# Stage transposes of the first tile ahead of the last group, mixers begun tile by tile, last rows in two operations, last down matrices by output columns

## The chip, the cores and the metric

The kernel runs on one core of a Trainium2 chip. The metric is the device time of one execution in microseconds; the kernel before took 2252.16 us (median of three runs, 2251.80 to 2252.19). The profiled execution took 2251.79 us, and its span from first to last instruction is 2249.9 us.

## What is computed

The network works on 256 tokens of 1024 values, in float32. First comes one block with 16 extra tokens: a gated linear attention and a latent attention side by side, an output projection, then a layer of 64 experts with two chosen per token. After it come two more layers, each a mixer and two feed-forward networks (FFN) around layer norms:

```python
h = h + hier_moe(rmsnorm(h, ffn_norm[l]), ...)      # 64 experts, hdn = silu(xb @ w_gate[e]) * (xb @ w_up[e]); hdn @ w_down[e]
return rmsnorm(h, final_norm)[:, N_META:]
...
def layer_norm(x, g, b):
    mu = jnp.mean(xf, -1, keepdims=True)
    var = jnp.mean(jnp.square(xf - mu), -1, keepdims=True)
    y = (xf - mu) * lax.rsqrt(var + LN_EPS)
    return (y * g + b).astype(x.dtype)
def swiglu(x, w_gate, w_up, w_down):
    return (jax.nn.silu(x @ w_gate) * (x @ w_up)) @ w_down
```

The order is FFN 0, convolution mixer, FFN 1, FFN 2, mLSTM mixer, FFN 3. Each stage adds its output to a scaled residual and passes the sum through a layer norm. Each mixer has a cross-attention to 256 memory rows of its own, and its output projection takes the memory part and the mixer part together (`out_project`, four chunks of weights, the memory part's first).

## The kernel before, in words

The residual `h` stays on chip as two tiles of 128 tokens. Weights stream from HBM: in the expert layer into eight slots of 2 MB (`E.W`), afterwards into a ring of eight chunks of 1 MB (`X.ring`). SyncE issues all these loads in order; each waits until the chunk that used its slot is spent. Nothing is planned at run time: each engine has its instructions in the order of the source, and semaphores hold them together. A float32 matrix product counts as two instructions on TensorE in every view; a transpose counts as one.

**The expert layer** (L954 to L991) handles four experts at a time, 16 times: gate, up, down, then `combine`, which spreads the result to both token tiles. The last four down matrices arrive as four slices of the inner dimension (L99, L886), each 4 KB runs for the full 1024 output columns, and `out_of_slices` (L919) uses them as they land. ScalarE copies the result (L1048), TensorE combines it (L935), VectorE adds it to `h` (L1083), ScalarE squares and sums (L1656), VectorE scales (L2043). `early_sums` (L2032) makes VectorE form the first FFN's first two sets of weight sums ahead of the adds (L1784 to L1788, four operations each).

**A stage boundary** of stage j: VectorE adds TensorE's output to `h` and takes statistics (`merged`, L1721, after an FFN; `norm`, L1713, after a mixer), ScalarE takes the root (L1551), VectorE normalises the tile in two halves (`scaled`, L1687), TensorE transposes the eight 128 x 128 squares of the tile (`turn`, L1256), and VectorE and ScalarE each write four of them into `N.xT` with gain and bias (`spread`, L1695 and L1563). Only then does the next stage have its input. `rows` (L1708, L1709) applies gain and bias to `h` itself later.

**An FFN** (L1266) forms its products by seven products of half matrices instead of eight (p = 1 to 7), so it needs sums of weights (`weight_sums`) and of tokens (`token_sums`, L1802 to L1806, which need both tiles). Its order on TensorE: `turn(j, 0)`, `plain(0)` on tile 0 alone, `turn(j, 1)`, `plain(1)`, then wait for the token sums and `mixed(0)`. `plain` has 32 instructions, `mixed` 80. It ends with the down products; the last three chunks are taken product by product, in the order p = 1, 2, 6, 5, 3, 7, 4 (L1345). Tile 0 is complete with p = 3, tile 1 with p = 4.

**The mixers** wait for both tiles (`wait_x`, L1260), then run `group` (L1351): 32 instructions of 256 columns per chunk of weights. The mLSTM first has 32 narrow instructions for its gates (L1445). `out_project` (L1391) goes tile by tile and half by half through four chunks, 16 instructions each time. In the mLSTM, before it, 12 transposes (L1520) wait for VectorE's head norm, whose last input is the output gate that follows the last `token_group` (L1513).

## Time and profile before

| | |
|---|---|
| time, median of 3 | 2252.16 us |
| profiled execution | 2251.79 us, its span 2249.9 us |
| TensorE busy (PE) | 1843.9 us, 82% of the span |
| VectorE busy | 859.9 us, 38% |
| ScalarE busy | 214.2 us, 10% |
| chain that ended last | PE 62%, DMA 30%, SyncE's queue 3%, VectorE 3%, ScalarE 1% |
| longest in the chain | L1280 24%, L1307 11%, expert weights 10%, 10% and 9%, L1355 5% |

In a timeline row, the first number is the start in us from the start of the span, the second is how long the group lasts, and x says how many instructions it joins. What stands in brackets is how long the engine sat idle before it and what ended that. The clock column gives TensorE's granted clock as a share of 2.4 GHz: 1.00 is full, 0.50 is 1.2 GHz.

### The profile page before, as it was taken

The page shows a single profiled execution, that of the slowest core. Times are in us where ns is not written, and L with a number is a line of the kernel's source. Part 1 is how long each engine was busy: PE and PEld are TensorE (multiplying, and loading weights), DVE is VectorE, ACT ScalarE, POOL GpSimd, SP SyncE. Part 2 cuts the span into 40 slices and gives each one's busy share as a digit, 9 for nine tenths or more (in the row PEclk, how much of TensorE's full clock was granted, in tenths as well). Part 3 has the DMA queues.
Part 4 walks back from the last instruction along what each step waited for, and adds up shares of the span by engine and source line. Part 5 has one row for each costly group of instructions (what it writes and reads, how often), then busy time and mean ns, then how long its engine had stood idle before and what let it go on. Part 6 is the DMA issues. An engine that isn't in the chain of part 4 may idle for free.

```text
span 2249.9 us, 26172 instructions
## 1 busy us (share of the span) xinstructions
PE 1843.9 (82%) x11372; PEld 1225.0 (54%) x11372; DVE 859.9 (38%) x1804; ACT 214.2 (10%) x409; POOL 17.9 (1%) x41
## 2 busy tenths in 40 slices
PE   8997665566665556656699999999999999989997
PEld 6754232222222222212399658699579947859973
DVE  2223111111011111110276742476776755347675
ACT  2321000000000000000100011000010002201000
POOL 1100000000000000000000000000000000000000
PEclk9998887888887888777899999999999999999999
DMA  9268999999999999999955443365545444315540
GB/s 275 71 244 346 427 427 428 427 428 428 428 424 428 427 428 428 428 428 427 361 173 182 174 160 122 118 200 184 172 150 180 177 150 150 113 59 185 181 186 27
DMA packets 185419, 604.64 MB, mean 269 GB/s; under 512 B 17805, under 2 KB 139079, under 8 KB 161239
## 3 DMA queue, kind: packets, MB, share of 16 engines
q1 hardware_dynamic: 179680, 595.51, 68.4%
q10 hardware_dynamic: 5623, 7.42, 1.0%
q8 instruction: 92, 1.51, 0.3%
q14 instruction: 24, 0.20, 0.0%
HBM read 601.86 MB, written 1.05 MB: 268 GB/s over the span
## 4 chain that ended last, share of the span: by engine, by line
PE 62%; DMA 30%; SPq 3%; DVE 3%; issue 1%; ACT 1%; ACTq 0%; DVEq 0%
PE banks L1280 24%; PE banks L1307 11%; DMA e_W<-in_expert_w_up 10%; DMA e_W<-in_expert_w_down 10%; DMA e_W<-in_expert_w_gate 9%; PE banks L907 6%; PE banks L1355 5%; PE banks L915 3%; PE banks L1399 2%; PE banks L1475 2%; PE banks L203 2%; SPq L144 1%; SPq L887 1%; DMA x_ring<-in_ffn_w_up 1%; PE banks L398 1%
## 5 line engine op out<-in xcount | busy, mean ns | idle before, releaser
L907 PE MATMUL banks<-e_W,e_xT 128*32 128x512 f32 x2048 | 284.8, 716 | 176.5 <-DMA e_W<-in_expert_w_up 87.6
L907 PEld LDWEIGHTS banks<-e_W,e_xT 128*32 128x32 f32 x2048 | 79.4, 129 | 370.0 <-issue 368.7
L915 PE MATMUL banks<-e_W,e_hT 128*32 128x512 f32 x960 | 139.2, 745 | 140.0 <-DMA e_W<-in_expert_w_down 140.0
L1280 PE MATMUL banks<-x_xs,x_sums 128*128 128x128 f32 x2112 | 243.0, 275 | 0.0
L1280 PEld LDWEIGHTS banks<-x_xs,x_sums 128*128 128x128 f32 x2112 | 239.4, 192 | 0.0
L1280 PE MATMUL banks<-x_xT,x_ring 128*128 128x128 f32 x1408 | 169.0, 280 | 8.5 <-DVE x_xT L1695 6.8
L1280 PEld LDWEIGHTS banks<-x_xT,x_ring 128*128 128x128 f32 x1408 | 164.9, 196 | 9.5 <-DVE x_xT L1695 7.5
L915 PEld LDWEIGHTS banks<-e_W,e_hT 128*32 128x32 f32 x960 | 38.2, 133 | 230.3 <-issue 230.3
L1083 DVE TENSOR_TENSOR c_h<-c_h,banks 128x1024 f32<-128x1024 f32 x32 | 39.0, 1221 | 312.3 <-PE banks L935 312.3
L1307 PE MATMUL banks<-x_sums,x_hs 128*128 128x512 f32 x264 | 125.0, 592 | 0.0
L1355 PE MATMUL banks<-x_xT,x_ring 128*128 128x256 f32 x544 | 122.0, 386 | 1.6 <-DVE x_xT L1695 1.6
L1079 DVE TENSOR_TENSOR e_xT<-banks,e_fng 128x512 f32<-128x512 f32 x32 | 20.6, 686 | 255.5 <-PE banks L895 255.5
L1355 PEld LDWEIGHTS banks<-x_xT,x_ring 128*128 128x128 f32 x544 | 104.7, 194 | 17.4 <-DVE x_xT L1695 1.9
L1107 DVE TENSOR_TENSOR e_hid<-e_act,banks 128x512 f32<-128x512 f32 x16 | 11.0, 688 | 234.7 <-PE banks L907 234.7
L1280 PE MATMUL banks<-x_xT,x_sums 128*128 128x128 f32 x704 | 86.2, 276 | 2.6 <-DVE x_xs L1806 2.6
L1280 PE MATMUL banks<-x_xs,x_ring 128*128 128x128 f32 x704 | 85.8, 275 | 0.0
L1307 PEld LDWEIGHTS banks<-x_sums,x_hs 128*128 128x128 f32 x264 | 50.2, 190 | 63.1 <-issue 63.1
L1280 PEld LDWEIGHTS banks<-x_xT,x_sums 128*128 128x128 f32 x704 | 82.1, 192 | 3.4 <-DVE x_xs L1806 3.4
L1280 PEld LDWEIGHTS banks<-x_xs,x_ring 128*128 128x128 f32 x704 | 82.1, 192 | 0.0
L1307 PE MATMUL banks<-x_ring,x_hT 128*128 128x512 f32 x176 | 81.4, 592 | 0.0
L1824 DVE TENSOR_TENSOR x_us<-x_p,banks 128x256 f32<-128x256 f32 x44 | 18.5, 421 | 156.3 <-PE banks L1280 156.3
L935 PE MATMUL banks<-e_y,e_mixT 128*128 128x512 f32 x128 | 59.2, 605 | 18.3 <-ACT e_y L1048 17.1
(466 smaller groups left out, 2027.5 us busy)
## 6 DMA issues: line engine op xcount, KB each, us to landing
e_W<-in_expert_w_gate SPq DMA_DIRECT2D x64, 2048.0 KB, 21.7
e_W<-in_expert_w_up SPq DMA_DIRECT2D x64, 2048.0 KB, 20.7
e_W<-in_expert_w_down SPq DMA_DIRECT2D x64, 2048.0 KB, 20.2
x_ring<-in_ffn_w_gate SPq DMA_DIRECT2D x44, 1024.0 KB, 5.4
x_ring<-in_ffn_w_up SPq DMA_DIRECT2D x44, 1024.0 KB, 7.6
x_ring<-in_ffn_w_down SPq DMA_DIRECT2D x44, 1024.0 KB, 5.1
x_ring<-in_w_in_mlstm SPq DMA_DIRECT2D x13, 1024.0 KB, 5.2
x_ring<-in_w_in_conv SPq DMA_DIRECT2D x10, 1024.0 KB, 5.2
```

Source lines behind the costliest of these rows:

```text
L144: sp.dma_start(dst, src).then_inc(ld["params"], 16)
L203: i = pe.matmul(o, lhs(k), rhs(k), start=(k == 0), stop=(k == KD - 1))
L398: pe.matmul(ps[:, 4 + 2 * t + n, :], M.yT[:, k, t * P:(t + 1) * P], K.wout[:, k, n * 512:(n + 1) * 512], start=(k == 0), stop=False)
L907: i = pe.matmul(ps[SLOT * j:SLOT * (j + 1), b, :], E.xT[:, x, k, SLOT * j:SLOT * (j + 1)], E.W[:, slot0 + j, k * DE:(k + 1) * DE], start=( ...
L915: i = pe.matmul(ps[SLOT * j:SLOT * (j + 1), 2 + c, :], E.hT[:, f, SLOT * j:SLOT * (j + 1)], E.W[:, slot0 + j, f * D + c * 512:f * D + (c + ...
L935: i = pe.matmul(ps[:, 6 - 2 * t + c, :], E.mixT[:, x, t, :], E.y[:, c * 512:(c + 1) * 512], start=True, stop=True)
L1083: return v.tensor_tensor(K.h[:, t, :], K.h[:, t, :], ps[:, 6 - 2 * t:8 - 2 * t, :].rearrange("p b n -> p (b n)"), ALU.add)
L1280: mm = pe.matmul(ps[:, bank, lo + which * P:lo + (which + 1) * P], a, b, start=(k == 0), stop=(k == 3))
L1307: mm = pe.matmul(ps[:, DB[p], :], a, b, start=(c == 0), stop=(c == NFC - 1))
L1355: mm = pe.matmul(ps[:, bank, f2 * S:(f2 + 1) * S], w8(i)[:, k, f2 * P:(f2 + 1) * P], N.xT[:, k, :], start=(k == 0), stop=(k == KD - 1))
L1399: mm = pe.matmul(yb(t, m), X.mixT[:, 2 * kk + k2, t * P:(t + 1) * P], w2(at + n)[:, k2, m * 512:(m + 1) * 512], start=(n == 0 and k2 == 0) ...
L1475: mm = pe.matmul(ps[:, bank, t * FC:(t + 1) * FC], N.xT[:, k, t * P:(t + 1) * P], w8(i)[:, k, :], start=(k == 0), stop=(k == KD - 1))
```

## The change

- `expert_chunk`: each of the last four down loads covers two of the four inner slices and half of the output columns, as two transfers with runs of 2 KB. `out_of_slice` finishes columns 0 to 511 first; copy, `combine_half`, add and square follow per half. `early_sums` is gone; those two sets of weight sums now stand behind `spread(0, 0)` and `spread(0, 1)`.
- `turn` of the next stage's tile 0 stands ahead of the very last down product (FFN) or ahead of the last quarter of the output projection (mixers). VectorE's order follows: `spread(j, 0)` before the last add. It works for FFNs 0 to 2.
- `conv` and `lstm` start with `tile_group` on tile 0 (32 instructions of 128 columns), then transpose tile 1, then do the second half. The gates go tile by tile too.
- `out_project` is split: `out_memory` (the memory part, 16 instructions for all four outputs) and `out_rest` (48). In the mLSTM `out_memory` stands ahead of the 12 transposes.
- `last_rows` replaces `scaled` and `rows` at the end: two operations on each half of a tile, each half stored at once.
- Six more products on the identity in the front, after the first transposes; the gate bias is loaded with two transfers.

```diff
-        return K.dram["expert_w_down"][0, QUAD * q:QUAD * (q + 1)].rearrange("e (p k) n -> p e k n", p=P)[:, :, j % QUAD, :]
+        return K.dram["expert_w_down"][0, QUAD * q:QUAD * (q + 1)].rearrange("e (p k) n -> p e k n", p=P)[:, :, 2 * (j % 2):2 * (j % 2) + 2, 512 * (j % QUAD // 2):512 * (j % QUAD // 2 + 1)]
...
+        for n in range(WARM // 2):
+            pe.matmul(ps[:, 7, 0:P], K.ident[:, :], K.ident[:, :], start=True, stop=True)
...
-                out_of_slices(at + 2 * QUAD)
+                pe.wait_ge(self.mix_out, QUADS)
+                for m in range(2):
+                    for f2 in range(2):
+                        out_of_slice(at + 2 * QUAD + 2 * m + f2, m, f2)
+                    pe.wait_ge(self.y_out, q + m + 1)
+                    combine_half(q % 2, m)
+                return
...
                     for c in range(NFC - TAIL, NFC):
                         if p == 6:
                             wait_down(c)
+                        if p == 4 and c == NFC - 1 and n < 3:
+                            turn(j + 1, 0)
                         down(c, p)
...
+            def out_rest(at, tail, j):
+                for t in range(TT):
+                    for m in range(2):
+                        if t == 1 and m == 1:
+                            turn(j, 0)
+                        for n in range(1, 4):
...
             def conv():
                 at = AT_CONV
-                for k in (0, 4):
-                    wait_x(1, k)
-                group(at, 0)
+                first_tile(1)
+                tile_group(at, 0, 0)
+                turn(1, 1)
+                both_tiles(1)
+                tile_group(at, 0, 1).then_inc(s["spent"], 1)
...
             def lstm():
+                first_tile(4)
+                gates(0)
+                tile_group(at, 1, 0)
+                turn(4, 1)
+                both_tiles(4)
+                gates(1)
+                tile_group(at, 1, 1).then_inc(s["spent"], 1)
...
                 pe.wait_ge(ls["va"], 3)
+                pe.wait_ge(ls["hv"], 1)
+                out_memory(at + 13, 1)
                 for t in range(TT):
                     pe.wait_ge(ls["y"], t + 1)
...
             def norm(j, scale, last):
+                summed(j, 0, 0, scale, last)
+                summed(j, 0, 1, scale, last)
                 scaled(j, 0)
-                sums(j, 1, scale, last)
+                summed(j, 1, 0, scale, last)
                 spread(j, 0)
+                summed(j, 1, 1, scale, last)
                 scaled(j, 1)
                 spread(j, 1)
...
                 v.bn_aggr(N.mv[:, 0, :], N.stats[:, 0, :, :]).then_inc(s["mv"], 1)
+                if j < 6:
+                    scaled(j, 0)
+                else:
+                    last_rows(0)
                 got(6)
                 after(z)
                 z = add(1, 1, prod(7))
-                scaled(j, 0)
                 y = add(1, 0, prod(7))
-                after(z)
-                stats(1, 1)
+                if j < 6:
+                    spread(j, 0)
                 v.wait_ge(s["spent"], last)
                 after(y)
-                c(add_last(1, 0, prod(4), scale))
+                x = add(1, 0, prod(4))
+                stats(1, 1)
+                after(x)
...
+            def last_rows(t):
+                v.wait_ge(moe.ld_rows, 16 + 32 * 6)
+                v.wait_ge(s["root"], TT * 5 + t + 1)
+                c(v.reciprocal(N.root[:, t:t + 1], N.root[:, t:t + 1]))
+                cols = [slice(m * 512, (m + 1) * 512) for m in range(2)]
+                centred = [K.vc.mark(v.scalar_tensor_tensor(out=h[:, t, m], in0=h[:, t, m], scalar=N.mv[:, t, 0:1], in1=N.g[:, m],
+                                                            op0=ALU.subtract, op1=ALU.mult)) for m in cols]
+                for m, n in zip(cols, centred):
+                    v.wait_ge(K.vc.sem, n)
+                    v.scalar_tensor_tensor(out=h[:, t, m], in0=h[:, t, m], scalar=N.root[:, t:t + 1], in1=N.b[:, m],
+                                           op0=ALU.mult, op1=ALU.add).then_inc(s["rows"], 1)
...
             spread(0, 0)
+            v.wait_ge(moe.spent, XCHUNKS)
+            weight_sums(0, 0)
             spread(0, 1)
+            weight_sums(0, 1)
```

## Rows read from the trace of the kernel before

**Rows 1.** Chain that ended last, in order of time: start us, us, what
```profile
1126.56 130.69 PE banks L1280 x1168
...
1353.82 3.65 PE banks L1363 x16
...
1357.47 14.01 PE banks L1355 x64
...
1411.77 27.48 PE banks L1399 x64
...
1451.33 130.69 PE banks L1280 x1168
...
1894.40 3.65 PE banks L1363 x16
...
2041.68 130.69 PE banks L1280 x1168
```

**Rows 2.** One line of the program (L1256, stage transposes): idle TensorE time, us and times
```profile
  DVE c_h L1687: 13.5, 7
```

**Rows 3.** Timeline around the second FFN's end: start us, us, engine line op tiles [idle before]
```profile
1645.37 2.74 PE L1307 MATMUL banks<-x_sums,x_hT 128*128 128x512 f32 x6
...
1646.37 1.00 DVE L1687 TENSOR_SCALAR c_h<-c_h,n_mv,n_root 128x512 f32<-128x512 f32 x2
...
1647.95 1.04 PE L1256 MATMUL banks<-c_ident,c_h 128*128 128x128 f32 x8
...
1649.02 1.50 ACT L1563 ACTIVATE x_xT<-banks,n_lnT 128x128 f32<-128x128 f32 x4 [4.03 <-PE banks L1256]
...
1651.42 3.84 PE L1280 MATMUL banks<-x_xT,x_ring 128*128 128x128 f32 x32 [2.44 <-DVE x_xT L1695]
...
1655.10 1.04 PE L1256 MATMUL banks<-c_ident,c_h 128*128 128x128 f32 x8
...
1660.45 1.72 PE L1280 MATMUL banks<-x_xT,x_sums 128*128 128x128 f32 x13 [0.75 <-DVE x_xs L1806]
```

**Rows 4.** Busy time per stretch (PE, PEld, DVE, ACT, POOL), TensorE clock, DMA share, GB/s
```profile
1330.00:1332.00 2.00, 1.94 (x5) 1.62 (x6) 1.97 (x3) 0.00 (x0) 0.00 (x0) 0.50 1.12 351
...
1862.00:1864.00 2.00, 1.04 (x5) 0.64 (x3) 1.77 (x5) 0.92 (x3) 0.00 (x0) 0.50 1.10 347
...
2032.00:2034.00 2.00, 2.00 (x12) 2.00 (x11) 0.07 (x1) 0.00 (x0) 0.00 (x0) 0.51 1.11 353
```

**Rows 5.** Timeline, transposes of tile 0 ahead of the convolution and the mLSTM
```profile
1323.18 1.04 PE L1256 MATMUL banks<-c_ident,c_h 128*128 128x128 f32 x8
...
1857.08 1.04 PE L1256 MATMUL banks<-c_ident,c_h 128*128 128x128 f32 x8
```

**Rows 6.** Timeline, before the mLSTM's output projection
```profile
1980.30 0.64 DVE L2012 BATCH_NORM_AGGREGATE x_hmv<-x_hst 128x2 f32<-128x6 f32 x8
...
1996.75 2.79 PE L1520 MATMUL banks<-c_ident,x_pad 128*128 128x128 f32 x12 [7.51 <-DVE x_pad L2021]
...
1999.58 0.69 DVE L2024 COPY x_mixT<-banks 128x512 f32<-128x512 f32 x1 [0.26 <-PE banks L1520]
```

**Rows 7.** Timeline: three VectorE operations in a row; last one of the kernel
```profile
1316.26 1.89 DVE L1722 SCALAR_TENSOR_TENSOR c_h<-x_ud,c_h 128x512 f32<-128x512 f32 x3
...
2245.61 1.22 DVE L1709 TENSOR_TENSOR c_h<-c_h,x_b 128x1024 f32<-128x1024 f32 x1
```

**Rows 8.** Clock, DMA share, GB/s: w_out (4 KB rows), w_kv (2 KB rows)
```profile
52.00:54.00 2.00, 1.00 1.01 412
...
98.00:100.00 2.00, 1.00 1.04 393
```

**Rows 9.** Timeline, end of the expert layer
```profile
1100.75 3.33 PE L924 MATMUL banks<-e_W,e_hT 128*32 128x512 f32 x16 [3.18 <-DMA e_W<-in_expert_w_down]
...
1109.06 2.34 DVE L1083 TENSOR_TENSOR c_h<-c_h,banks 128x1024 f32<-128x1024 f32 x2
...
1115.35 6.38 PE L1280 MATMUL banks<-x_xT,x_ring 128*128 128x128 f32 x32 [1.71 <-DVE x_xT L1697]
```

More of the change, by code:

```diff
@@ L1110, in vector @@
             if q == QUADS - 1:
-                early_sums()
+                for m in range(2):
+                    cols = slice(m * 512, (m + 1) * 512)
+                    for t in range(TT):
+                        v.wait_ge(self.c_mm, TT * (q + m) + t + 1)
+                        v.tensor_tensor(K.h[:, t, cols], K.h[:, t, cols], ps[:, 6 - 2 * t + m, :], ALU.add).then_inc(self.summed, 1)
+                return
             for t in range(TT):
@@ L1245, in _ @@
             for t in range(TT):
-                sp.wait_ge(s["rows"], 7 * TT - TT + t + 1)
-                sp.dma_start(out[t * P:(t + 1) * P, :], h[:, t, :]).then_inc(s["stored"], 16)
-            sp.wait_ge(s["stored"], 16 * TT)
+                for m in range(2):
+                    sp.wait_ge(s["rows"], 6 * TT + 2 * t + m + 1)
+                    sp.dma_start(out[t * P:(t + 1) * P, m * 512:(m + 1) * 512], h[:, t, m * 512:(m + 1) * 512]).then_inc(s["stored"], 16)
+            sp.wait_ge(s["stored"], 16 * 2 * TT)
         @block.tensor
@@ L1357, in group, with tile_group @@
                 mm.then_inc(s["spent"], 1)
+            def tile_group(i, bank, t):
+                if t == 0:
+                    wait_chunk(pe, i)
+                for f2 in range(2):
+                    for k in range(KD):
+                        mm = pe.matmul(ps[:, bank, f2 * S + t * P:f2 * S + (t + 1) * P], w8(i)[:, k, f2 * P:(f2 + 1) * P],
+                                       N.xT[:, k, t * P:(t + 1) * P], start=(k == 0), stop=(k == KD - 1))
+                return mm
             def scores(layer):
@@ L1389, in turn_o, with out_part, out_memory @@
                 i.then_inc(xs["xy_mm"], 1)
-            def out_project(at, tail):
+            def out_part(at, n, t, m):
+                for k2 in range(2):
+                    mm = pe.matmul(yb(t, m), X.mixT[:, 2 * OUT_K[n] + k2, t * P:(t + 1) * P], w2(at + n)[:, k2, m * 512:(m + 1) * 512],
+                                   start=(n == 0 and k2 == 0), stop=(n == 3 and k2 == 1))
+                if t == 1 and m == 1:
+                    mm.then_inc(s["spent"], 1)
+                elif n == 3:
+                    mm.then_inc(s["bank"], 1)
+            def out_memory(at, layer):
+                wait_chunk(pe, at)
+                pe.wait_ge(xs["xy_out"], layer + 1)
                 for t in range(TT):
                     for m in range(2):
-                        for n, kk in enumerate(OUT_K):
+                        out_part(at, 0, t, m)
+            def out_rest(at, tail, j):
+                for t in range(TT):
+                    for m in range(2):
+                        if t == 1 and m == 1:
+                            turn(j, 0)
+                        for n in range(1, 4):
                             if t == 0 and m == 0:
@@ L1525, in tail @@
                         pe.wait_ge(ls["y_out"], TT)
-                out_project(at + 13, tail)
+                out_rest(at + 13, tail, 5)
             front.tensor(pe)
@@ L1530, in _ @@
             ffn(0, 0)
-            for t in range(TT):
-                turn(1, t)
             conv()
@@ L1535, in _ @@
             ffn(2, 3)
-            for t in range(TT):
-                turn(4, t)
             lstm()
@@ L1653, in _ @@
             moe.scalar(a)
-            for t in range(TT):
-                a.wait_ge(moe.summed, TT * (QUADS - 1) + t + 1)
-                K.ac(a, a.activation(N.junk[:, :], h[:, t, :], ACT.Square, accum_out=N.ss[:, t:t + 1]))
-                a.activation(N.root[:, t:t + 1], N.ss[:, t:t + 1], ACT.Sqrt, bias=K.eps[:, 0:1], scale=1.0 / D).then_inc(s["sumsq"], 1)
             spread(0, 0)
@@ L1702, in rows @@
                 for t in range(TT):
[L1703 to L1706 removed]
+                    v.wait_ge(s["turned"], 4 * j + 2 * t + 2)
                     if j:
@@ L1761, in merged @@
                 if j < 6:
-                    spread(j, 0)
-                scaled(j, 1)
-                if j < 6:
+                    scaled(j, 1)
                     spread(j, 1)
+                else:
+                    last_rows(1)
+            def last_rows(t):
[9 more added lines that the diff above has]
+                                           op0=ALU.mult, op1=ALU.add).then_inc(s["rows"], 1)
             def add_last(t, m, x, scale):
@@ L2051, in _ @@
             ffn(3, 5)
-            rows(6)
         @block.gpsimd
```

135 lines of the change are left out of this document (69 added, 66 removed).

## The prediction

> **What bounds the kernel now.** I read the chain of work that ended last first, because it says which engine sets the end in each stage. Up to 1089 us it is the stream of expert weights. From there on it is TensorE almost without a break, in long pieces such as the 130.69 us of FFN products [rows 1]. So the kernel can only be shortened where that chain of products is cut: at the stage boundaries and before the mLSTM's projection. The view of one line of the program says what the stage transposes waited for: 13.5 us of idle TensorE time in front of them, ended by VectorE's normalisation [rows 2]. The timeline shows how a boundary looks. After FFN 1 the last product row (p = 4) starts at 1645.37, the transposes of tile 0 at 1647.95, ScalarE's spread ends at 1650.52, and `plain(0)` starts only at 1651.42, because VectorE did tile 1's sums before its own spread [rows 3]. The last view is the one by stretches: at three of the boundaries the granted clock was 0.50 of 2.4 GHz [rows 4], so a boundary costs more than its idle time.
>
> **The units.** A 512-column instruction takes 27.48 / 64 = 0.43 us, so one down product (two instructions) takes 0.86 us and an output projection 27.5 us [rows 1]. A `group` of 32 instructions with 256 columns takes 14.01 / 2 = 7.0 us [rows 1]. 32 instructions with 128 columns take 3.65 us: 1651.42 to 1655.10 [rows 3] is that with the turn to the next work. So `tile_group` twice costs 7.3 us where `group` cost 7.0: splitting a group costs only 0.3 us. From the start of a `turn`, with the spreads free to run, to the end of ScalarE's spread it is 1650.52 - 1647.95 = 2.57 us, and I take 2.62 until TensorE goes on [rows 3]. From `turn(j, 1)` to `mixed(0)` it is 1660.45 - 1655.10 = 5.35 us [rows 3], set by spread and token sums and unchanged.
>
> **FFN 1 to FFN 2.** Call the old start of tile 0's transposes A. In the new order they start at A - 0.86, ahead of the last product, which then runs beside the spread. They wait for `scaled(j, 0)`. VectorE now does it as soon as the root is there and no longer after an add, and even in the old order it began at 1646.37, in two halves of 0.5 us [rows 3]. The transposes would start at 1647.09, and the second half is ready about 1646.5. The new wait is covered by about 0.6 us; if it were late, only the last product and the spread would queue behind it. `plain(0)` then starts at A - 0.86 + 2.62 = A + 1.76 instead of A + 3.47. Gain **1.7 us**. Tile 1 is late next: add, two statistics, root, scaling end about 7.9 us after 1645.37, and its transposes come 8.1 us after it, so they do not wait.
>
> **FFN 0 to the convolution.** A is 1323.18 [rows 5]. First half at A + 1.76, then 3.65, the turn of tile 1 with its wait 2.62, second half 3.65, two groups 13.96: the memory scores start at A + 25.64 = 1348.8. Before they started at 1353.82 [rows 1]. Gain **5.0 us**, of which about 3.1 us is the clock: the first fifteen instructions ran at 1.2 GHz [rows 4]. I take it that the new waits (0.7 and 1.6 us instead of 3.1 and 1.6) leave the clock at 2.4 GHz.
>
> **FFN 2 to the mLSTM.** A is 1857.08 [rows 5]. A + 1.76, then gates and `tile_group` of tile 0 (3.65 each; the trace has the gates only at 256 columns, and their 32 instructions cannot take longer than those of `tile_group`), 2.62, again 3.65 twice, two groups 13.96: the scores start at A + 32.9 = 1890.0 instead of 1894.40 [rows 1]. Gain **4.4 us**, some 2.9 of it clock [rows 4]. `rows(4)` on VectorE starts later but is over before the first queries are wanted.
>
> **Convolution to FFN 1.** The projection's work stays (27.5). Tile 0's transposes (1.04) stand in it, waiting for a normalisation that has a whole quarter (12 x 0.43 = 5.2 us) against the 3.7 us it needs. Then `plain(0)` 3.75 and 5.35 follow without a gap: 37.6 us from 1411.77, where it was 1451.33 - 1411.77 = 39.56 [rows 1]. Gain **2.0 us**.
>
> **The end of the mLSTM** is the largest term. TensorE sat idle 7.51 us in front of the 12 transposes, which took 2.79 us at half clock [rows 6]. `out_memory` is 16 x 0.43 = 6.9 us of work that fits into this gap, from 1989.24 to 1996.1. Its new wait on the head statistics is over at 1980.94 [rows 6]. The transposes start at 1996.75 as before, since the head norm hangs on the last `token_group` alone, and last 1.6 us. VectorE's copies, which ended at 1999.58 + 1.0 [rows 6], end about 1999.9; before, the memory part covered them, now TensorE waits some 1.5 us. Then 48 x 0.43 = 20.6, transposes 1.0, `plain(0)` 3.75, 5.35: `mixed(0)` at 2030.6 instead of 2041.68 [rows 1]. Gain **11.0 us**: 6.9 for the filled gap, 2.2 for clock up to 2001, 1.6 for clock in `plain(0)` [rows 4], 1.9 for the boundary, less 1.5 for the uncovered copies.
>
> **The end.** VectorE's last operation ended at 2245.61 + 1.22 = 2246.83 [rows 7]. Two operations on halves replace two on halves and two on whole tiles, and tile 0 no longer stands behind tile 1. Three such operations lasted 1.89 us, so four take 2.5 [rows 7]. `last_rows(0)` now delays tile 1's adds: its statistics are complete about 1.0 us later (2241.5), root and reciprocal 0.55, four operations 2.5: 2244.6. Gain 2.2; storing halves makes the last transfer half as large, up to 0.7 more. I take **2.7 us**.
>
> **The end of the expert layer.** The pieces become 2 KB instead of 4 KB. 4 KB rows moved at 412 GB/s and 2 KB rows at 393 [rows 8], a mean of 388 with the stretch after it; for 8.4 MB I add 1.4 us, between 0 and 2.5. By the Trainium skill (DMA: Bandwidth & Descriptors, Specifications) pieces from 512 B on reach line rate; then these 1.4 us are not paid and the total is 2223.9. In the other direction the work behind the last slice is halved: it ended with VectorE's adds at 1109.06 + 2.34 = 1111.40 [rows 9]. Now: products until 1104.1 + 1.4 [rows 9], copy of half the columns about 0.65, four products 1.9 with their latency, an add 0.7: 1108.8, so `plain(0)` starts 2.6 us earlier, at 1112.75 instead of 1115.35 [rows 9]. But the weight sums that ran during the wait for the last slice now stand behind the spreads. The first set (four operations, 2.6 by [rows 7]) hides behind `plain(0)`; the second stands between spread and token sums and delays `mixed(0)` by 2.6. The two cancel: gain **0.0**. With `plain(0)` at full clock instead of 1.2 GHz (6.38 us against 3.75) it is 2.6 more. With a drop caused by the new wait of 2.5 us before `mixed(0)` it is about 3 less.
>
> **At nothing:** the six products in the front (what follows waits for parameters until 47 us), the bias transfers, the earlier memory part in the convolution.
>
> Sum: 1.7 + 5.0 + 4.4 + 2.0 + 11.0 + 2.7 + 0.0 = 26.8 us. 2251.79 - 26.8 = 2225.0; the median of the runs is 0.37 higher, so **2225.3 us**.
>
> **The rivals.**
> *The clock still falls* at the two mixer starts. For it: it fell in [rows 4] after boundaries with 2.2 to 3.1 us of idle time, and 1.6 us remain, with 1.04 us of transposes before them. Against it: the boundary of [rows 3] had 2.44 us idle after transposes and ran on at full speed. Price 3.1 + 2.9: 2231.3 us. The Trainium skill (TensorE: Matmul & The Clock Gate, Part 4) says transposes do not count as busy time; by that the pause at tile 1's turn is 2.7 us and not 1.6, which is the argument for this rival. Chance 0.12.
> *The expert tail keeps its clock*, 2222.7 us: chance 0.15. *It loses it before `mixed(0)`*, 2228.3 us: chance 0.18. Both come from the same row [rows 9].
> *The memory part does not fill the gap*, because the head norm moves with it: 2232.2 us. Against it: no operation of that norm reads what `out_memory` writes. Chance 0.04.
> *Slower than before:* SyncE cannot feed eight transfers of 4096 pieces fast enough, and the last slice lands late. Everything behind it moves by the same amount, so this decides from 26.8 us on: 8.4 MB in 48 us, 175 GB/s. The 2 KB row at 393 speaks against it [rows 8]. At 160 GB/s the kernel would take 2256 us. Chance 0.03, with 0.01 for a loss that just cancels the gain.
>
> **How the numbers follow.** The forecast as it stands has 0.47, with 2 us either way for the small terms. The range 2221 to 2231.5 takes in the two cases of the expert tail and most of the first rival. A measurement of this kernel tells 0.2%, 4.5 us, from no change. All cases but the last give more than that: faster 0.96, same 0.01, slower 0.03.
>
> **What would show it.** TensorE's idle time before the 12 transposes of L1520 falls from 7.5 to under 1 us and they last 1.6; the clock stays at 1.00 in the first 10 us of both mixers; `plain(0)` follows the last output quarter without a gap; the last VectorE operation ends some 2.2 us earlier against p = 4's start; `mixed(0)` of FFN 0 starts within 1 us of 1126.6. The prediction is wrong if the new turns wait for VectorE, or if a 128-column half takes clearly more than 3.7 us.

## The result, and the profile after

The changed kernel takes **2218.66 us** (median of four runs, 2217.18 to 2219.77), the kernel before beside it 2252.18 us (2251.80 to 2252.26). The ratio is 0.985, with a 95% interval from 0.984 to 0.9864. That is 33.5 us faster; 26.8 were forecast, and 2218.66 lies 2.3 us below the low end of the range. The profiled execution took 2217.64 us with a span of 2215.9 us, 34.0 us less than the span before.

The chain of work that ended last, in order of time, of the kernel after (start us, us, what):

```profile
1122.20 130.69 PE banks L1322 x1168
...
1344.64 3.65 PE banks L1416 x16
...
1402.60 22.32 PE banks L1446 x52
...
1439.70 130.69 PE banks L1322 x1168
...
1647.15 130.69 PE banks L1322 x1168
...
1873.39 3.65 PE banks L1416 x16
...
2009.25 130.69 PE banks L1322 x1168
```

L1322 is `mixed(0)`, L1416 the memory scores, L1446 the output projection. Set against [rows 1] these starts cut the 34.0 us into parts. The start of `mixed(0)` in FFN 2 before was 1660.45 [rows 3].

| stretch | before | after | gain | forecast |
|---|---|---|---|---|
| start to `mixed(0)` of FFN 0 | 1126.56 | 1122.20 | 4.4 | 0.0 |
| to the convolution's scores | 227.26 | 222.44 | 4.8 | 5.0 |
| to its output projection | 57.95 | 57.96 | 0.0 | 0 |
| to `mixed(0)` of FFN 1 | 39.56 | 37.10 | 2.5 | 2.0 |
| to `mixed(0)` of FFN 2 | 209.12 | 207.45 | 1.7 | 1.7 |
| to the mLSTM's scores | 233.95 | 226.24 | 7.7 | 4.4 |
| to `mixed(0)` of FFN 3 | 147.28 | 135.86 | 11.4 | 11.0 |
| to the end of the span | 208.22 | 206.65 | 1.6 | 2.7 |

Two terms are far off: the expert tail (4.4 us too little) and the mLSTM's start (3.3 too little). The others differ by +0.5, +0.4, 0.0, -0.2 and -1.1.

The timeline of the kernel after at the start of the mLSTM (start us, us, engine line op tiles, idle time before in brackets):

```profile
1842.92 1.04 PE L1296 MATMUL banks<-c_ident,c_h 128*128 128x128 f32 x8
...
1843.79 1.02 PE L1349 MATMUL banks<-x_sums,x_hT 128*128 128x512 f32 x2
...
1845.64 1.92 PE L1507 MATMUL banks<-x_xT,x_wgate 128*4 128x128 f32 x32 [0.83 <-ACT x_xT L1631]
...
1847.49 3.84 PE L1408 MATMUL banks<-x_xT,x_ring 128*128 128x128 f32 x32
...
1851.16 1.04 PE L1296 MATMUL banks<-c_ident,c_h 128*128 128x128 f32 x8
...
1853.89 1.92 PE L1507 MATMUL banks<-x_xT,x_wgate 128*4 128x128 f32 x32 [1.69 <-ACT x_xT L1631]
```

The transposes (L1296) wait for nothing, the last down product (L1349) runs beside the spread, and the two waits that remain are 0.83 and 1.69 us. But the gates (L1507) take 1.92 us a tile, where the forecast had 3.65. The same timeline before the mLSTM's output projection:

```profile
1968.12 7.03 PE L1446 MATMUL banks<-x_ring,x_mixT 128*128 128x512 f32 x16
1975.76 1.74 PE L1592 MATMUL banks<-c_ident,x_pad 128*128 128x128 f32 x12 [0.61 <-DVE x_pad L2102]
1978.77 7.53 PE L1446 MATMUL banks<-x_ring,x_mixT 128*128 128x512 f32 x17 [1.26 <-DVE x_mixT L2106]
```

Where TensorE sat idle for 7.51 us [rows 6] it now does the memory part, and the 12 transposes take 1.74 us in place of 2.79. The view by stretches shows the clock there and at both mixers (columns as in [rows 4]):

```profile
1318.00:1320.00 2.00, 1.87 (x11) 1.04 (x9) 1.70 (x6) 0.96 (x3) 0.00 (x0) 1.00 0.72 217
1324.00:1326.00 2.00, 1.33 (x13) 1.09 (x11) 1.07 (x4) 0.63 (x2) 0.00 (x0) 1.00 1.04 351
1330.00:1332.00 2.00, 2.00 (x15) 1.84 (x14) 1.82 (x3) 0.00 (x0) 0.00 (x0) 1.00 0.04 8
1850.00:1852.00 2.00, 2.00 (x20) 1.96 (x19) 0.20 (x1) 0.00 (x0) 0.00 (x0) 1.00 1.10 349
...
1976.00:1978.00 2.00, 1.51 (x12) 1.04 (x10) 1.90 (x4) 0.00 (x0) 0.00 (x0) 1.00 0.72 204
```

All are at 1.00, full speed; the slow stretches of [rows 4] were at 0.50 and 0.51. At the convolution the two waits that remain are 0.78 and 1.69 us:

```profile
1320.65 3.81 PE L1408 MATMUL banks<-x_xT,x_ring 128*128 128x128 f32 x32 [0.78 <-DVE x_xT L1760]
...
1327.02 3.81 PE L1408 MATMUL banks<-x_xT,x_ring 128*128 128x128 f32 x32 [1.69 <-ACT x_xT L1631]
```

### The profile page after: what moved, and what is told of

Its sections match the earlier page's. It is cut to its first block, busy times and chain, and to the rows that moved or that the text cites. A ratio compares the mean times of both kernels' runs of the same rounds, so it can differ in the third digit from the quotient of the medians.

```text
span 2215.9 us, 26410 instructions
## 1 busy us (share of the span) xinstructions
PE 1828.5 (83%) x11480; PEld 1219.8 (55%) x11480; DVE 860.1 (39%) x1806; ACT 216.1 (10%) x416; POOL 17.8 (1%) x41
## 4 chain that ended last, share of the span: by engine, by line
PE 63%; DMA 29%; SPq 4%; DVE 2%; issue 1%; ACT 1%; DVEq 0%; ACTq 0%
PE banks L1322 24%; PE banks L1349 12%; DMA e_W<-in_expert_w_gate 10%; DMA e_W<-in_expert_w_down 9%; DMA e_W<-in_expert_w_up 9%; PE banks L913 7%; PE banks L1399 5%; PE banks L921 3%; PE banks L1446 2%; PE banks L1545 2%; PE banks L203 2%; SPq L144 1%; SPq L893 1%; SPq L891 1%; PE banks L1408 1%
## 5 line engine op out<-in xcount | busy, mean ns | idle before, releaser
L1322 PE MATMUL banks<-x_xs,x_sums 128*128 128x128 f32 x2112 | 243.0, 275 | 0.0
L1322 PEld LDWEIGHTS banks<-x_xs,x_sums 128*128 128x128 f32 x2112 | 239.4, 192 | 0.0
L1322 PE MATMUL banks<-x_xT,x_ring 128*128 128x128 f32 x1408 | 166.2, 277 | 2.1 <-DVE x_xT L1762 1.3
L1322 PEld LDWEIGHTS banks<-x_xT,x_ring 128*128 128x128 f32 x1408 | 162.5, 194 | 4.1 <-DVE x_xT L1760 1.6
L1349 PE MATMUL banks<-x_sums,x_hs 128*128 128x512 f32 x264 | 125.0, 592 | 0.0
L1399 PE MATMUL banks<-x_xT,x_ring 128*128 128x256 f32 x480 | 105.2, 380 | 0.0
L1399 PEld LDWEIGHTS banks<-x_xT,x_ring 128*128 128x128 f32 x480 | 90.6, 190 | 12.6 <-issue 0.7
L1322 PE MATMUL banks<-x_xT,x_sums 128*128 128x128 f32 x704 | 86.2, 276 | 4.5 <-DVE x_xs L1887 4.5
L1322 PE MATMUL banks<-x_xs,x_ring 128*128 128x128 f32 x704 | 85.8, 275 | 0.0
L1322 PEld LDWEIGHTS banks<-x_xT,x_sums 128*128 128x128 f32 x704 | 82.1, 192 | 5.3 <-DVE x_xs L1887 5.3
L1349 PEld LDWEIGHTS banks<-x_sums,x_hs 128*128 128x128 f32 x264 | 50.2, 190 | 63.1 <-issue 63.1
L1322 PEld LDWEIGHTS banks<-x_xs,x_ring 128*128 128x128 f32 x704 | 82.1, 192 | 0.0
L1349 PE MATMUL banks<-x_ring,x_hT 128*128 128x512 f32 x176 | 81.4, 592 | 0.0
## 6 DMA issues: line engine op xcount, KB each, us to landing
e_W<-in_expert_w_up SPq DMA_DIRECT2D x64, 2048.0 KB, 21.3
e_W<-in_expert_w_down SPq DMA_DIRECT2D x60, 2048.0 KB, 21.3
```

What stands on the lines that cost most here:

```text
L1322: mm = pe.matmul(ps[:, bank, lo + which * P:lo + (which + 1) * P], a, b, start=(k == 0), stop=(k == 3))
L1349: mm = pe.matmul(ps[:, DB[p], :], a, b, start=(c == 0), stop=(c == NFC - 1))
L1399: mm = pe.matmul(ps[:, bank, f2 * S:(f2 + 1) * S], w8(i)[:, k, f2 * P:(f2 + 1) * P], N.xT[:, k, :], start=(k == 0), stop=(k == KD - 1))
```

## The experiments

Twelve series of runs were made: ten kernels that differ from the changed one or from the one before by a single piece (one of them by two), one of these a second time, and the changed kernel again. Each stands beside the kernel before on the same chip (2251.8 to 2252.4 us in the median). Where a distance in a trace is given, it comes from one profiled execution of each kernel. "Landing" is the start of the products of the last down slice. Nothing of the computation is left out in any of them.

### The gates without alternating strips

`gates` writes its two halves to partitions 0 to 3 and 32 to 35, and takes them in turn. One edit puts the two halves one behind the other:

```diff
                 def gates(t):
-                    for k in range(KD):
-                        for f2 in range(2):
+                    for f2 in range(2):
+                        for k in range(KD):
```

> The changed kernel, with one loop order turned round: the mLSTM's gate products of a tile do all eight inner slices for the input gates (output rows 0 to 3) and then all eight for the forget gates (rows 32 to 35), where the changed kernel alternates between the two. Theory: they took 1.92 us for 32 instructions because neighbours in the queue write different row strips and run side by side; in a row on one strip they take 3.65 us for each tile, 3.5 us more in all, about 2222.2 us. Rival: 128 columns with four weight columns are cheap in any order; then 1.92 us again and 2218.7 us.

2222.71 us (2220.73 to 2224.24), ratio 0.9873 [0.9858, 0.9888]. That is 4.0 us more than the changed kernel; from `mixed(0)` of FFN 2 to the scores its trace has 2.6 more (228.85 against 226.24), and the rest is no more than the runs spread. Its timeline:

```profile
1846.20 3.22 PE L1507 MATMUL banks<-x_xT,x_wgate 128*4 128x128 f32 x32 [0.83 <-ACT x_xT L1631]
...
1855.75 3.22 PE L1507 MATMUL banks<-x_xT,x_wgate 128*4 128x128 f32 x32 [1.69 <-ACT x_xT L1631]
```

The same 32 instructions take 3.22 us one behind the other and 1.92 us alternated, 0.100 and 0.060 us each. A product of 128 columns on the full array takes 0.114 us per instruction (3.65 / 32), so 0.060 us is less than one takes by itself: products that write different strips of partitions overlap. The theory holds in kind, but serial they take 3.22 us and not the 3.65 expected. The forecast missed the overlap, and the trace of before had it. There the experts' products go to four strips at L907:

```profile
182.11 7.07 PE L907 MATMUL banks<-e_W,e_xT 128*32 128x512 f32 x64 [1.03 <-DVE e_xT L1079]
```

64 instructions of 512 columns take 7.07 us, where the output projection's 64 take 27.48 [rows 1]. The Trainium skill (TensorE: Matmul & The Clock Gate, Part 3: Packing small matmuls) says that products on different 32-wide strips of the array run concurrently; the trace agrees in kind, with a factor of 1.68 for two strips.

### The expert tail in its old form

All of the tail is put back: slices of inner rows, one add per tile, `early_sums`. The core of the edit:

```diff
-        return K.dram["expert_w_down"][...][:, :, 2 * (j % 2):2 * (j % 2) + 2, 512 * (j % QUAD // 2):512 * (j % QUAD // 2 + 1)]
+        return K.dram["expert_w_down"][...][:, :, j % QUAD, :]
...
             if q == QUADS - 1:
-                for m in range(2):
-                    cols = slice(m * 512, (m + 1) * 512)
...
-                return
+                early_sums()
```

> The changed kernel with the whole end of the expert layer as it was: four slices of 4 KB runs, copy and combine of full width, both weight sums before the adds. The prediction's step: the two orders cost the same, 2218.7 us plus nothing. The theory after the result: the new order is worth 3 to 4 us here, half of it because TensorE's clock stays up in the last slice; 2222.3 us. Rival: only the phase of the clock differed between the two traces, and the difference is under 1 us.

2223.25 us (2222.86 to 2223.32), ratio 0.9872 [0.9857, 0.9888]: 4.6 us more than the changed kernel. So the two orders do not cost the same, and the rival of under 1 us falls.

```profile
1081.11 9.60 PE L909 MATMUL banks<-e_W,e_xT 128*32 128x512 f32 x64 [10.44 <-DMA e_W<-in_expert_w_up]
...
1101.44 1.92 PE L926 MATMUL banks<-e_W,e_hT 128*32 128x512 f32 x16 [3.06 <-DMA e_W<-in_expert_w_down]
1104.51 3.70 PE L937 MATMUL banks<-e_y,e_mixT 128*128 128x512 f32 x8 [1.14 <-ACT e_y L1050]
```

The last slice landed 1101.44 - 1081.11 = 20.33 us after the start of the last `up` products. In the kernel after it is 1101.19 - 1079.89 = 21.30, by the rows further down. From landing to `mixed(0)` it is 25.39 us here, 25.81 in the kernel before and 21.01 after. So the new order lands 1.0 us later and is 4.4 us shorter behind that, 3.4 together; the other 1.2 us between the two traces lie ahead of the last `up`, where the kernels are alike. The reason expected for half of the gain was wrong: the last products take 1.92 us here too, at full clock.

### The old tail with 2 KB runs

Beside the edit above:

```diff
+                for m in range(2):
+                    sp.dma_start(dst[:, :, m * 512:(m + 1) * 512], expert_chunk(K, c)[:, :, m * 512:(m + 1) * 512])...
+                continue
             sp.dma_start(dst, expert_chunk(K, c)).then_inc(E.arrived[c % SLOTS], 16)
```

> The expert's last down matrices in their old order (by rows), with each of the four last slices loaded as two transfers whose runs are 2 KB long in place of one with 4 KB: the pieces of the new order without the new order. With 4 KB runs the last slice landed 20.28 to 20.35 us after the start of the last up products, in the new order 21.29 to 21.40. Theory: the length of the runs makes the 1.0 us, so here it lands after 21.3 us and the kernel takes 2223.3 to 2224.3 (the old order with 4 KB runs took 2223.25). Rival: the 1.0 us comes from the order or from what is issued around it; then it lands after 20.3 us again and the time stays at 2223.2.

```profile
1082.13 9.78 PE L912 MATMUL banks<-e_W,e_xT 128*32 128x512 f32 x64 [10.25 <-DMA e_W<-in_expert_w_up]
...
1103.54 2.56 PE L929 MATMUL banks<-e_W,e_hT 128*32 128x512 f32 x16 [3.36 <-DMA e_W<-in_expert_w_down]
```

Landing 21.41 us after `up`. Over all fourteen profiles it is 20.28 to 20.35 us with 4 KB runs and 21.28 to 21.41 with 2 KB runs, in either order. So the 2 KB runs, with the twice as many transfers that they come in here, make the 1.0 us, and the rival falls; the two were not separated. The time, 2225.54 us (2222.28 to 2227.36), is above the expected 2224.3, but its four runs lie 5 us apart, so only the landing in the trace carries the verdict.

### The weight sums first

VectorE's second set of weight sums of FFN 0 is placed ahead of `spread(0, 1)`:

```diff
             weight_sums(0, 0)
-            spread(0, 1)
             weight_sums(0, 1)
+            spread(0, 1)
```

> The changed kernel, with the second set of weight sums of FFN 0 ahead of VectorE's spread of tile 1, not behind it. Theory: VectorE sat idle for 3.47 us before that spread and TensorE then waited 2.27 us for the token sums; the set (2.6 us) fits into the idle time, mixed(0) starts 1.9 us earlier, about 2216.8 us. If TensorE's wait before mixed(0) is also what makes runs differ by 2.3 us, the runs lie within 1 us of each other. Rival: the set's weights land later than the idle time and spread waits for them; then no gain or a loss up to 2 us.

It ran in two series. The first:

2217.64 us (2211.86 to 2219.46), ratio 0.9839 [0.9825, 0.9852].

```profile
1122.16 2.05 PE L1322 MATMUL banks<-x_xT,x_sums 128*128 128x128 f32 x16 [0.39 <-DVE x_xs L1887]
```

The wait ahead of `mixed(0)` falls from 2.27 to 0.39 us. The runs did not come closer together, so that wait is not what spreads them. Nor did this execution start `mixed(0)` sooner than the changed kernel's (1122.16 against 1122.20): its `plain(0)` took 6.50 us in place of 5.47 and its last slice landed 0.8 us later.

> The kernel with the weight sums of VectorE ahead of the additions alone, beside the changed kernel and the one with both edits. It gave 2217.64 us (2211.86 to 2219.46), while the wait that it takes away is 1.9 us. Theory: in the same job it lies 1 to 2 us under the changed kernel, 2216.5 to 2218. Rival: the wait was worth nothing, since plain(0) takes its place by going slower; then both are within 0.5 us.

> The changed kernel itself, unaltered, so that the two kernels that build on it are compared with it on the same chip. It gave 2218.66 us in the median of four runs, from 2217.18 to 2219.77. Theory: 2218.0 to 2219.3 again, with single runs up to 2 us apart, since the stretch in which the granted clock falls among the mLSTM's small attend products costs more in some executions than in others. Rival: the spread came from the first job; then the runs lie within 0.5 us.

The text above on this kernel, and the one below on both edits, put the sums ahead of the additions; the edit is the one shown, ahead of `spread(0, 1)`. Side by side the changed kernel took 2218.07 us (2216.87 to 2219.37), as expected, and this one 2214.95 (2213.68 to 2219.70), below the expected 2216.5 to 2218. Over both series that is a mean of 2218.4 for nine runs against 2216.0 for ten: 2.4 us, where the wait is 1.9. The ten spread over 7.8 us, so the mean alone is weak. The traces are firmer: from landing to `mixed(0)` it is 21.01 us in the changed kernel and 19.12 in the second profile with the sums first, with `plain(0)` at 5.47 and 5.46 us. The second profile of the changed kernel shows something else at this place (timeline of that run):

```profile
1109.40 3.84 PE L1322 MATMUL banks<-x_xT,x_ring 128*128 128x128 f32 x32 [1.33 <-DVE x_xT L1762]
...
1119.96 2.61 PE L1322 MATMUL banks<-x_xT,x_sums 128*128 128x128 f32 x16 [2.27 <-DVE x_xs L1887]
```

Here `plain(0)` runs at full clock (3.84 us) and the clock falls behind the wait of 2.27 us; `mixed(0)` takes 132.32 us in the chain and not 130.69. In the first profile it is the other way round: 5.47 us, and no fall behind the wait. The forecast had these as two separate rivals. They are two outcomes of one kernel, and here each costs 1.6 us. They don't exclude each other: the profile of the kernel without the six products (its run is further down) has both, `plain(0)` in the timeline and `mixed(0)` in the chain.

```profile
1110.53 5.26 PE L1320 MATMUL banks<-x_xT,x_ring 128*128 128x128 f32 x32 [1.33 <-DVE x_xT L1760]
...
1122.51 132.32 PE banks L1320 x1168
```

And in the profile with the last rows as they were, `plain(0)` took 6.67 us, with the same code up to there.

### Both waits away

With the edit above, GpSimd multiplies the output gate third by third:

```diff
-            g.wait_ge(ls["og"], 3)
-            for t in range(TT):
-                i = g.tensor_tensor(X.og[:, t, :], X.og[:, t, :], X.hg[:, :], ALU.mult)
+            for n in range(3):
+                g.wait_ge(ls["og"], n + 1)
+                for t in range(TT):
+                    w = slice(n * FC, (n + 1) * FC)
+                    i = g.tensor_tensor(X.og[:, t, w], X.og[:, t, w], X.hg[:, w], ALU.mult)
```

> Two waits of the changed kernel are taken away. The weight sums of VectorE stand ahead of the last down products' additions, so that TensorE waits 0.4 us and not 2.27 ahead of mixed(0) of FFN 0. And GpSimd multiplies the output gate by the head gain third by third, as each arrives, and not in one piece behind the last, so that it is mostly done when VectorE takes the last third's 8 products of 192 columns (3.91 us now). Theory: 1.9 us for the first and up to 0.6 us for the second (the wait ahead of the 12 transposes), 2216.2 to 2216.8 where the changed kernel gives 2218.7, and VectorE's 8 operations take 2.0 to 2.5 us because GpSimd no longer works beside them. Rival: GpSimd isn't the cause of the 0.49 us of one such operation; then they take 3.9 us as before, the wait stays at 0.6 us and the time is 2216.8 to 2217.4.

One line of the program (L2098, VectorE) in the kernel after, then in this one (duration in ns as min/median/max):

```profile
L2098 DVE TENSOR_SCALAR x_pad<-x_pad,x_hmv,x_hrs x8: 368/370/1881, 1970.8 to 1974.3; 128x192 f32<-128x192 f32 x8
```
```profile
L2098 DVE TENSOR_SCALAR x_pad<-x_pad,x_hmv,x_hrs x8: 374/375/381, 1975.7 to 1977.7; 128x192 f32<-128x192 f32 x8
```

In the kernel after, one of the eight operations lasts 1.88 us, about as long as GpSimd's second multiplication beside it (1.81 us); the other seven take 0.37. With GpSimd done before they begin (its last multiplication ends at 1975.31), all take 0.38, so the rival falls. The Trainium skill (SBUF — State Buffer, Who interferes with whom) says that a VectorE operation of this kind can share a pair of ports with GpSimd, that the pair is an exclusive lock, and that the one that comes second stands until the other is done; the trace agrees. The 12 transposes now follow without a wait, and from the last `token_group`'s start to `mixed(0)` of FFN 3 it is 53.95 us in place of 54.78: 0.8 us.

The time is 2216.80 us (2213.30 to 2221.91), ratio 0.9835 [0.9822, 0.9849]. That is below the changed kernel, but these runs spread most of all, and against the edit of the sums alone no gain can be read from the times. Both faster variants stand on their traces: a wait of 1.9 us gone, and 0.8 us before FFN 3.

### The turns in their old places

```diff
-                        if p == 4 and c == NFC - 1 and n < 3:
-                            turn(j + 1, 0)
...
-                        if t == 1 and m == 1:
-                            turn(j, 0)
```

with `turn` at the head of each stage, and VectorE's `spread(j, 0)` after the last add.

> The changed kernel with the transposes of tile 0 and VectorE's spread back behind the last group of each stage; mixers still begin tile by tile. Theory (the boundary terms of the prediction): about 1.7 us for each of the three FFN boundaries and 2.0 for each of the two mixer boundaries come back, 9 us, 2227.8 us, and more if the clock falls to 1.2 GHz at a boundary. Rival: VectorE's order and not TensorE's sets the boundary, and under 4 us come back.

2232.71 us (2230.91 to 2234.96), ratio 0.992 [0.9904, 0.9937]: 14 us lost, of which its trace shows 11.9 at the boundaries; 9 and more were expected, and the rival of under 4 falls. At the convolution, then at the mLSTM:

```profile
1324.32 3.84 PE L1405 MATMUL banks<-x_xT,x_ring 128*128 128x128 f32 x32 [2.58 <-DVE x_xT L1757]
...
1855.35 2.97 PE L1503 MATMUL banks<-x_xT,x_wgate 128*4 128x128 f32 x32 [2.58 <-DVE x_xT L1757]
1858.26 4.39 PE L1405 MATMUL banks<-x_xT,x_ring 128*128 128x128 f32 x32
```

Both waits are 2.58 us. At the convolution the half group behind it runs at full clock, 3.84 us. At the mLSTM the gates take 2.97 us in place of 1.92 and the half group 4.39 in place of 3.84: the clock fell. The five stretches lose 1.8 (convolution), 2.4, 1.8, 3.4 and 2.5 us; at the other four, `plain(0)` or the half group behind the wait took 3.84 us, full clock.

### The mixers with whole groups

```diff
-                first_tile(1)
-                tile_group(at, 0, 0)
                 turn(1, 1)
                 both_tiles(1)
-                tile_group(at, 0, 1).then_inc(s["spent"], 1)
+                group(at, 0)
```

and likewise in the mLSTM, with both gates behind `turn(4, 1)`.

> The changed kernel with both mixers waiting for both tiles before their first group (transposes of tile 0 stay early; the gates still go by tiles). Theory: convolution and mLSTM each start 3.5 to 5.5 us later against tile 0 and pay 0.3 us less for the split group; with the clock at 2.4 GHz 2218.7 + 3.3 + 5.2 = 2227 us. If the clock falls during the wait for tile 1, as it did in the kernel before, 3 us more at each: up to 2233 us. The rival of the prediction (the clock falls at the mixers although they begin by tiles) would make it differ by the waiting time alone.

2228.77 us (2227.88 to 2229.46), ratio 0.9901 [0.9884, 0.9917], 10.1 us lost, inside the expected 2227 to 2233. Its trace puts 5.8 us on the convolution and 4.6 on the mLSTM.

```profile
1854.30 1.50 PE L1296 MATMUL banks<-c_ident,c_h 128*128 128x128 f32 x8 [3.42 <-DVE c_h L1748]
1857.49 5.64 PE L1505 MATMUL banks<-x_xT,x_wgate 128*4 128x128 f32 x64 [1.69 <-ACT x_xT L1627]
```

With nothing to do between the two turns TensorE waits 3.42 us, and what follows runs slower: the transposes take 1.50 us where they take 1.04 at full clock. At the convolution it is a wait of 3.33 us and transposes of 1.97. So in these executions it is the half group between the two turns, and not the earlier turn, that kept the clock up at the convolution.

### The memory part alone

Here the kernel before gets this one piece of the change:

```diff
                 pe.wait_ge(ls["va"], 3)
+                pe.wait_ge(ls["hv"], 1)
+                out_memory(at + 13)
...
-                out_project(at + 13, tail)
+                out_project(at + 13, tail, 1)
```

> The kernel before with one edit: the memory part of the mLSTM's output projection stands ahead of the 12 transposes. The prediction's terms: 6.9 for the gap, 2.2 for the clock, less 1.5 for the copies that nothing covers, and up to 1.6 if the clock stays up at the next boundary: 2252.2 - 7.6 = 2244.6 us, down to 2243.0. Rival (the head norm moves with it): 2252 us.

2243.78 us (2242.74 to 2245.50), ratio 0.9966 [0.9953, 0.9978]: about 8 us by itself.

```profile
1990.24 7.03 PE L1396 MATMUL banks<-x_ring,x_mixT 128*128 128x512 f32 x16
1997.89 1.75 PE L1531 MATMUL banks<-c_ident,x_pad 128*128 128x128 f32 x12 [0.61 <-DVE x_pad L2032]
2000.90 20.84 PE L1408 MATMUL banks<-x_ring,x_mixT 128*128 128x512 f32 x48 [1.26 <-DVE x_mixT L2036]
```

The three rows have the durations and waits of the kernel after. The gap is filled, and the copies stand uncovered for 1.26 us as foreseen. From the start of the last `token_group` to `mixed(0)` of FFN 3 the trace has 58.78 us where the kernel before has 66.26: 7.5 us, for 7.6 worked out.

### The last rows and the six products

For the last rows, `scaled(6, t)` and `rows(6)` are put back, with whole-tile stores.

> The changed kernel with the last rows as they were (scaled and rows on whole tiles, two stores). The prediction's term: 2.7 us come back, 2221.4 us. What the trace showed: 1.6 us, 2220.3 us.

2221.78 us (2219.29 to 2223.40), ratio 0.9865 [0.9849, 0.9882]. From `mixed(0)` of FFN 3 to the end it is 208.72 us: 2.1 more than after, between the two expectations. The median is 3.1 more, but the four runs lie 4 us apart. Without the six products on the identity:

> The changed kernel without the six added products on the identity in the front. The prediction's step: they cost and give nothing, 2218.7 us. Rival: the 0.57 us by which the expert layer began earlier in the changed kernel is theirs; 2219.2 us.

2217.78 us (2216.88 to 2219.40), ratio 0.9847: they neither cost nor bring anything that can be measured, as forecast.

## Why the prediction was wrong, step by step

**Right.** What bounds the kernel, where it can be cut, and the mechanism of each piece. The moved turns did not wait for VectorE anywhere. FFN 1 to FFN 2 gave 1.7 us as worked out. The convolution gave 4.8 for 5.0, with waits of 0.78 and 1.69 us where 0.7 and 1.6 were worked out. The end of the mLSTM came to 11.4 for 11.0, down to the wait of 1.26 us for the copies. The rival of the falling clock at the mixers fell: from `mixed(0)` to the scores it is 222.4 and 226.2 us in every profile with the new order and the alternating gates (1.6 more where the clock fell in `mixed(0)` itself). `mixers_whole` shows the other side: in waits of 3.33 and 3.42 us the clock fell. The length of the wait alone does not decide it: 2.58 us in `turns_old` kept the clock at the convolution and lost it at the mLSTM, and ahead of FFN 3 a wait of 2.18 us kept it in `turns_old` (`plain(0)` 3.84 us) and lost it in `memory_part_alone` (5.40 us). The rule of the Trainium skill that the prediction set beside this rival (TensorE: Matmul & The Clock Gate, Part 4) makes the pause at tile 1's turn 1.04 us of transposes plus 1.69 of waiting; the clock held through it, so here it decided nothing.

**The step that failed first: the gates** (3.5 us of the 7.2 by which the sum was short of the spans' 34.0). The prediction said that "their 32 instructions cannot take longer than those of `tile_group`" and then put this upper bound of 3.65 us into the sum as if it were the value. Serial they take 3.22, alternated 1.92, as `gates_serial` shows: over both tiles 0.9 us of the 3.5 is that the bound was loose, and 2.6 is the alternation. The kernel before did its two halves one behind the other on the same partitions (L1445). The change puts them on partitions 32 x f2 in turn, which its list does not name and the forecast left out, though the code and L907's row had it. The serial figure could be read too: at clock 1.00 the trace of before has 21 of the gates' instructions in the 4 us from 1870.00, 0.19 us for 256 columns, by which 32 of 128 columns take some 3.1 us (an estimate).

**The second: the expert tail** (4.4 us). The "two cancel" set 2.6 us won ahead of `plain(0)` against 2.6 us lost behind it. Measured, `plain(0)` starts 5.3 us earlier (1110.02 for 1115.35), is itself 0.9 us shorter, and the loss is 1.9. The last `up` of the kernel before, then the timeline of the kernel after:

```profile
1080.40 8.41 PE L907 MATMUL banks<-e_W,e_xT 128*32 128x512 f32 x64 [9.92 <-DMA e_W<-in_expert_w_up]
```
```profile
1079.89 8.73 PE L913 MATMUL banks<-e_W,e_xT 128*32 128x512 f32 x64 [9.63 <-DMA e_W<-in_expert_w_up]
...
1101.19 1.92 PE L930 MATMUL banks<-e_W,e_hT 128*32 128x512 f32 x16 [2.06 <-DMA e_W<-in_expert_w_down]
...
1107.60 1.09 PE L1296 MATMUL banks<-c_ident,c_h 128*128 128x128 f32 x8 [1.73 <-DVE c_h L2119]
...
1110.02 5.47 PE L1322 MATMUL banks<-x_xT,x_ring 128*128 128x128 f32 x32 [1.33 <-DVE x_xT L1762]
...
1115.96 1.13 DVE L1762 TENSOR_SCALAR x_xT<-banks,n_lnT 128x128 f32<-128x128 f32 x4 [3.47 <-PE banks L1296]
...
1122.20 2.05 PE L1322 MATMUL banks<-x_xT,x_sums 128*128 128x128 f32 x16 [2.27 <-DVE x_xs L1887]
```

The 5.3 us, against [rows 9] and the forecast's chain:

- 2.6 were forecast.
- 1.4 more: the last products take 1.92 us and not 3.33, since the clock stays up. In the old order it fell in waits of 3.18 and 3.36 us ahead of them (3.33 and 2.56 us) and stayed up in waits of 2.66 and 3.06; in the new order the waits are 0.9 to 2.4 us, and it stayed up in all ten profiles.
- 0.4 more: the landing is 1.0 later and not 1.4. So the forecast's case in which 2 KB pieces cost nothing (2223.9) did not come either.
- 0.5 more: the last `up` starts at 1079.89 and not at 1080.40. Nothing was changed there but the front, and it starts between 1079.3 and 1085.1 in the profiles, so this is chance.
- 0.4 is left. It lies in the chain of half-size copies, adds and squares and was not split further.

`plain(0)` takes 5.47 us and not 6.38. That too is chance of the execution: with the same tail it took between 3.84 and 6.67 us. The second set of weight sums costs 1.9 and not 2.6, because part of it lies beside ScalarE's spread; that is the 2.27 - 0.39 us of the experiment with the sums first. From the start of the last `up` to `mixed(0)` it is 45.72, 46.16 and 46.20 us in the three profiles with the old tail and 4 KB runs. In the seven with the new tail as forecast it is 40.67 to 43.51, five of them 42.20 to 42.41. So the tail itself is worth some 3.3 to 4.0 us and not 0.0.

The better clock alone was not enough: in the old order with the last products at 1.92 us, landing to `mixed(0)` was still 25.39 us, since VectorE's early sums hold its adds until 1109.71. The combined rows of tile 0 are done at about 1106.5 there (an estimate: half of the 3.70 us from 1104.51). So up to 3 us of what is won ahead of `plain(0)` may come from moving the sums and not from the halves by columns. No run moves the sums alone, and this split stays open.

**The third, in the other direction: the end** (1.1 us too much).

```profile
2203.22 1.41 DVE L1841 SCALAR_TENSOR_TENSOR c_h<-c_h,n_mv,n_g 128x512 f32<-128x512 f32 x2
...
2203.30 2.74 PE L1349 MATMUL banks<-x_sums,x_hT 128*128 128x512 f32 x6
2204.55 1.41 DVE L1845 SCALAR_TENSOR_TENSOR c_h<-c_h,n_root,x_b 128x512 f32<-128x512 f32 x2
...
2211.35 1.41 DVE L1845 SCALAR_TENSOR_TENSOR c_h<-c_h,n_root,x_b 128x512 f32<-128x512 f32 x2
```

A set of four lasts from 2203.22 to 2205.96, 2.74 us, where 2.5 was taken from three operations in 1.89 [rows 7], and it is paid twice, since tile 0's set stands ahead of tile 1's adds; these three take 2.08 and not 1.89. VectorE's last operation ends 9.46 us after the start of p = 4 (2203.30), forecast 8.87, before 11.10. The span ends 3.14 us after it and ended 3.07 after it before: storing halves gave none of the up to 0.7 us, of which the forecast counted 0.5.

**The range.** Both large errors were a bound and a difference taken as values, and both lay on the side of more gain. With half of 3.65 us left open for each of the gates' two halves, the low end would have been 3.65 lower, at 2217.4, and would have held the result. Of the 7.2 us by which the sum was short, 1.4 (the last `up` and `plain(0)`) are chance of the profiled execution.

**Left open.** Single runs of one kernel lie up to 8.6 us apart. Three stretches in the profiles move: the front (first expert products start between 180.7 and 186.6 us), the place of the clock's fall at FFN 0 (1.6 us), and the mLSTM's group behind its small products, whose 32 instructions take 7.10 us at full clock and up to 10.14. What decides in the front, and what decides whether the clock falls in a wait of 2.2 to 2.6 us, was not tried.

## What to carry to other kernels

A wait in front of TensorE costs its length and often slow instructions behind it too: fill it with a piece that is ready (the memory part, one tile's half of a group, the last product) rather than make what it waits for a little faster. When work is split to start earlier, ask of each small product which partitions it writes; two strips in alternation made 32 instructions cost 1.92 us instead of 3.22. And where two terms of a sum cancel, price every link of that chain from a row, since their difference is the least certain number of all.

## What the runs showed of the hardware that was not expected

- Products on two strips of partitions overlap in float32: 3.22 to 1.92 us for 32 instructions of 128 columns.
- Equal waits in the same kernel, 2.58 us ahead of each mixer in `turns_old`, kept the clock once and lost it once.
- One VectorE operation of 192 columns stood behind a GpSimd multiplication for its whole length: 1.88 us in place of 0.37.
- Loads of the same 8.4 MB in 2 KB runs instead of 4 KB ended 1.0 us later (21.3 to 21.4 us after `up` against 20.3), and SyncE's queue issued them in 19.30 us as eight transfers in place of 4.16 us as four.
- In one and the same kernel the clock fell at `plain(0)` in one execution and only behind the following wait of 2.27 us in another. A row that shows a fall in one profile doesn't say that it is there in each run.
- VectorE's four operations with a scalar per partition took 2.74 us for 4 x 512 values, 0.69 each; three with an immediate took 0.63 each [rows 7]. The wait between the pairs is not the reason: one operation by itself lasts 0.74 to 0.75 us with the scalar per partition (L1841, L1845) and 0.68 to 0.69 with the immediate (L1786). Whether the kind of scalar or what else the operations read makes it was not tried.
